# Two experts' outputs kept on chip and summed by one-hot products on TensorE, in a two-layer encoder step

## Chip, cores and metric

The kernel runs on one core of a Trainium2 chip, in one launch. The metric is the time of the program on the device in microseconds, measured before as the median of three runs.

## What is computed

Two layers over 576 rows of 1024 (512 prompt frames, 64 sample frames; padded to five row tiles of 128). Each layer is attention and a gated MLP in parallel, an output projection, a layer norm, a mixture of experts and a second layer norm. Only the experts and the norm behind them matter here. From the reference:

```python
combine = jnp.einsum('tk,tke->te', w, jax.nn.one_hot(idx, N_EXPERTS, dtype=jnp.float32))  # top 2 of 16
y = jnp.zeros_like(xt)
for e in range(N_EXPERTS):
    h = jax.nn.silu(xt @ wg[e]) * (xt @ wu[e])
    y = y + combine[:, e:e + 1] * (h @ wd[e])
...
x = layer_norm(ALPHA * x + y, ln2_g[l], ln2_b[l])
```

## The kernel before

**Products.** A float32 product with weights is made of three fast ones: ScalarE copies a weight unit to `w_hi` (`split_hi`), VectorE subtracts it into `w_lo` (`split_lo`), and TensorE multiplies hi by hi, hi by lo and lo by hi. Each layer has 108 units of up to 1 MB, loaded by SyncE into `raw` and `raw_far`. Products from `pe.matmul` with plain float32 operands (transposes, the gated MLP's) are single.

**Experts.** Each of the 16 experts has 128 places. POOL gathers an expert's rows from `x1_dram`; TensorE makes `gate`, `up` and `down`; ScalarE copies the output from banks C and D to `expert_out` (two buffers, by even and odd expert, `expert_rows_out`); POOL scatters it to `y2_dram` (`send`), row 2r + j for the j-th chosen expert of row r. `out_free` tells ScalarE when a buffer is free. Experts 1 to 14 run in a loop; expert 15 is last, with `down` of 14 and 15 behind it. Where an expert has more than 128 rows, further blocks run in `overflow`; every engine loads the count and branches there. In the profiled execution no block runs.

**Behind the experts**, in each layer:
- ScalarE: `h_hi` of expert 15, the test in `overflow`, in layer 0 splits of units 0 and 1 of the next layer (`next_split`), the last `expert_rows_out`, two more splits, then x times ALPHA for five tiles (`scaled`).
- VectorE: `h_lo` of expert 15, sums of the chosen scores and the weights `w12`, the test, in layer 0 the splits 0 to 2, then `add_first` for five tiles, `add_second` with the row sum, `centre_2` and `normalise` (a centre and a scale operation per tile); `x_ready` tells that a tile is finished.
- POOL: loads of `y_first` tiles 0 and 1 when the last unit is split, the scatter of expert 15, the other loads of `y_first`, and, when the scatter has landed, the loads of `y_second`.
- TensorE: `head(l + 1)`, in layer 0 only: turn a tile of x (`turn_rows`, banks E and F), wait for `xt_hi` and `xt_lo`, the first projection's product (24 instructions) of that tile.
- SyncE: the next layer's w_in, units 0 to 3 as places come free, units 4 on when `x_ready` has come for tile 0.

Banks are filled in a fixed order, which `fill_plan` writes down: a filler waits until the filling before it was read.

## Time and profile before

| what | us |
|---|---|
| median of 3 runs | 1206.39 |
| lowest, highest | 1197.67, 1210.31 |
| profiled execution | 1204.36 |
| its span | 1202.8 |
| busy in the span: TensorE, VectorE, ScalarE, POOL | 1060.8, 890.2, 710.1, 207.6 |

The mean granted clock of TensorE is 0.941 of full speed. The page's line of TensorE's clock over 40 slices of 30 us shows 9 or 8 tenths nearly everywhere, 5 in the slice from 571 us on (between the layers), and 8 and 5 in the last two. Times are read as microseconds from the span's start; layer 0 ends and layer 1 begins at about 571 to 593.

### The profile page before, as it was taken

To read this page: it belongs to the slowest core of one execution; us is meant where nothing else is said; L and a number is where in the kernel's file an instruction comes from. 1 tells how busy PE (TensorE), PEld (TensorE's weight loads), DVE (VectorE), ACT (ScalarE), POOL (GpSimd) and SP (SyncE) were. 2 spreads that over 40 slices of the span, in tenths; PEclk is the share of its full clock that TensorE was granted. 3 is DMA by queue.
4 is the path that set the end of the run, shared out by engine and by line. 5 is a ranking of instruction groups with operands and counts; after the bars stand their busy time and mean duration, and the time that the engine had idled before them with its cause. 6 is when DMAs were issued, how large, how long until landed. Compare 5 with 4: busy or idle time off the path is not lost.

```text
span 1202.8 us, 16880 instructions
## 1 busy us (share of the span) xinstructions
PE 1060.8 (88%) x5460; PEld 888.5 (74%) x5460; DVE 890.2 (74%) x1136; ACT 710.1 (59%) x871; POOL 207.6 (17%) x182
## 2 busy tenths in 40 slices
PE   5999799989989999999289987999799999999950
PEld 4987598877878888887178866888677888888840
DVE  2683865378979988887747737735899798888947
ACT  2423665265768887877433246723577787787852
POOL 3000000014632111210220000100173311222120
PEclk9999889998999999999589988999899999999985
DMA  9523111217999999997824212002499999999934
GB/s 301 160 77 105 51 38 44 88 72 275 356 358 380 388 382 377 381 379 278 251 72 166 61 62 88 27 18 105 134 308 360 378 389 383 379 383 384 378 122 151
DMA packets 117061, 273.26 MB, mean 227 GB/s; under 512 B 10305, under 2 KB 13345, under 8 KB 116993
## 3 DMA queue, kind: packets, MB, share of 16 engines
q1 hardware_dynamic: 98608, 227.36, 52.1%
q0 software_dynamic: 17088, 42.45, 10.6%
q10 hardware_dynamic: 1296, 2.62, 0.7%
q8 instruction: 33, 0.54, 0.2%
q14 instruction: 36, 0.29, 0.1%
HBM read 262.02 MB, written 25.22 MB: 239 GB/s over the span
## 4 chain that ended last, share of the span: by engine, by line
PE 52%; DMA 20%; DVE 10%; issue 6%; ACT 5%; POOL 3%; DVEq 2%; ACTq 0%; SPq 0%; POOLq 0%
DMA raw_far<-in_w_gate 14%; PE bankA L1666 9%; PE bankB L1666 7%; PE bankA L1915 7%; PE bankB L1915 5%; PE bankC L1666 4%; PE bankD L1666 4%; PE bankC L1938 3%; PE bankD L1938 3%; POOL slot_rows L673 3%; DVE w_lo L427 3%; PE bankG L1739 2%; ACT w_hi L421 2%; PE bankE L1655 2%; PE bankF L1655 1%
## 5 line engine op out<-in xcount | busy, mean ns | idle before, releaser
L427 DVE TENSOR_TENSOR w_lo<-raw,w_hi 128x2048 fp32r<-128x2048 f32 (+1 forms) x152 | 340.8, 2262 | 55.5 <-ACT w_hi L421 51.4
L421 ACT ACTIVATE w_hi<-raw 128x2048 fp32r<-128x2048 f32 (+1 forms) x152 | 287.4, 1896 | 138.7 <-PE bankC L1666 46.1
L427 DVE TENSOR_TENSOR w_lo<-raw_far,w_hi 128x2048 fp32r<-128x2048 f32 x64 | 146.4, 2288 | 15.3 <-ACT w_hi L421 15.3
L421 ACT ACTIVATE w_hi<-raw_far 128x2048 fp32r<-128x2048 f32 x64 | 122.8, 1919 | 50.3 <-PE bankB L1915 22.0
L1915 PE MATMUL bankA<-w_hi,xe_hi 128*128 128x512 f32 x256 | 101.8, 398 | 3.8 <-DVE xe_lo L442 3.6
L1915 PE MATMUL bankB<-w_hi,xe_hi 128*128 128x512 f32 x256 | 102.6, 401 | 1.3 <-DVE w_lo L427 1.3
L1915 PE MATMUL bankA<-w_lo,xe_hi 128*128 128x512 f32 x256 | 100.6, 393 | 0.0
L1915 PE MATMUL bankA<-w_hi,xe_lo 128*128 128x512 f32 x256 | 100.6, 393 | 0.0
L1915 PE MATMUL bankB<-w_hi,xe_lo 128*128 128x512 f32 x256 | 100.1, 391 | 0.0
L1915 PE MATMUL bankB<-w_lo,xe_hi 128*128 128x512 f32 x256 | 99.9, 390 | 0.0
L653 POOL DMA_INDIRECT y_rows<-expert_out,idx x32 | 53.2, 1662 | 173.4 <-ACT expert_out L928 171.0
L647 POOL DMA_INDIRECT rows<-x_rows,idx x24 | 37.0, 1541 | 219.6 <-PE bankF L1655 158.0
L1915 PEld LDWEIGHTS bankA<-w_hi,xe_hi 128*128 128x128 f32 x256 | 48.6, 190 | 18.1 <-DVE xe_lo L442 8.0
L1938 PE MATMUL bankC<-w_hi,h_hi 128*128 128x512 f32 x128 | 53.2, 415 | 4.9 <-DVE h_lo L442 4.9
L1915 PEld LDWEIGHTS bankA<-w_hi,xe_lo 128*128 128x128 f32 x256 | 48.6, 190 | 10.4
L1915 PEld LDWEIGHTS bankB<-w_hi,xe_hi 128*128 128x128 f32 x256 | 48.1, 188 | 10.8 <-DVE w_lo L427 1.8
L1915 PEld LDWEIGHTS bankA<-w_lo,xe_hi 128*128 128x128 f32 x256 | 48.6, 190 | 9.7
L1915 PEld LDWEIGHTS bankB<-w_hi,xe_lo 128*128 128x128 f32 x256 | 48.0, 188 | 10.3
L1915 PEld LDWEIGHTS bankB<-w_lo,xe_hi 128*128 128x128 f32 x256 | 48.2, 188 | 9.1
L1938 PE MATMUL bankC<-w_lo,h_hi 128*128 128x512 f32 x128 | 50.7, 396 | 0.0
L1938 PE MATMUL bankC<-w_hi,h_lo 128*128 128x512 f32 x128 | 50.6, 395 | 0.0
L1938 PE MATMUL bankD<-w_hi,h_hi 128*128 128x512 f32 x128 | 50.1, 391 | 0.0
(373 smaller groups left out, 2539.6 us busy)
## 6 DMA issues: line engine op xcount, KB each, us to landing
raw<-in_w_up SPq DMA_DIRECT2D x64, 1024.0 KB, 7.3
raw_far<-in_w_gate SPq DMA_DIRECT2D x60, 1024.0 KB
raw<-in_w_down SPq DMA_DIRECT2D x60, 1024.0 KB, 12.4
raw<-in_w_in SPq DMA_DIRECT2D x12, 1024.0 KB, 6.5
raw<-in_w_o SPq DMA_DIRECT2D x8, 1024.0 KB, 6.2
x_rows<-x POOLq DMA_DIRECT2D x10, 512.0 KB, 3.0
raw<-in_w_gate SPq DMA_DIRECT2D x4, 1024.0 KB
raw_far<-in_w_down SPq DMA_DIRECT2D x4, 1024.0 KB
```

What stands on the lines that cost most here:

```text
L421: act.activation(w_hi[:, s % RB, :, 0:n], raw_unit(s)[:, :, 0:n], ACT.Copy).then_inc(hi_done, 1)
L427: dve.tensor_tensor(w_lo[:, s % RB, :, 0:n], raw_unit(s)[:, :, 0:n], w_hi[:, s % RB, :, 0:n].bitcast(F32), ALU.subtract).then_inc(lo_done, 1)
L647: pool.indirect_dma_start(out=rows[:, e % 2, :], out_offset=None, in_=x1_dram, in_offset=bass.IndirectOffsetOnAxis(ap=src.bitcast(U32), ax ...
L653: pool.indirect_dma_start(out=y2_dram, out_offset=bass.IndirectOffsetOnAxis(ap=idx[:, e, 0:1].bitcast(U32), axis=0), in_=expert_out[:, e % ...
L673: pool.indirect_dma_start(out=slot_dram, out_offset=bass.IndirectOffsetOnAxis(ap=slots[:, c:c + 1].bitcast(U32), axis=0), in_=ints[:, c, : ...
L1655: ins = pe.transpose(bank_of(name)[:, k * P:(k + 1) * P], src, ident)
L1666: ins = pe.matmul(out, a[:, k, col:col + P], w[:, slot, j, 0:n], start=(m == 0 and a is a_hi and w is w_hi), stop=(m == len(steps) - 1 and ...
L1739: ins = pe.matmul(bank_of(("o", t))[:, h * 64:(h + 1) * 64], probs_t[:, j % 2, 2 * a + b, :], v[b], start=(b == (0 if t else 1)), stop=(b ...
L1915: ins = pe.matmul(out, a[:, 4 * k + t, (c % 2) * P:(c % 2 + 1) * P], w[:, (s + k) % RB, t, :], start=(k == t == 0 and a is xe_hi and w is ...
L1938: ins = pe.matmul(bank_of(f"down{h}")[:, :], a[:, 2 * j + r, cols], w[:, (s + j) % RB, 2 * r + h, :], start=(j == r == 0 and a is h_hi and ...
```

## The change

The outputs of experts 14 and 15 are not scattered. They stay in `expert_out`. VectorE makes, for both, a one-hot matrix of each row tile (`own`: a row's place in the expert, times its weight); TensorE turns these (`own_t`), and `own_sum(t)` multiplies them with the outputs into two banks per row tile. VectorE adds the banks to x (`add_own`). In x, rows in these two experts' first 128 places have weight 0 for the fetched output, and `y2_dram` is filled with the input rows ahead of each layer's experts, so that rows never scattered hold finite numbers. The other outputs are loaded by SyncE: `y_second` when the last `up` product is filled, `y_first` when the last unit is split. ScalarE scales x before the test. Row tiles' adds are now: second, first, own.

Cut to its core:

```diff
+    for name, bank in ((("own", 0), "E"), (("own", 1), "F"), (("own", 2), "H")):
+        fill(name, bank)
+    for t in range(NT):
+        for h in range(2):
+            fill(("sum", t, h), ("AB", "CD", "GH", "GH", "GH")[t][h])
     return at, count
...
-        y_second = over(base_m, "y_second", [P, NT, D], at=8 * HALF)
+        y_second = over(base_t, "y_second", [P, NT - 1, D], at=24576)
+        y_second_last = over(base_m, "y_second_last", [P, D], at=4 * D)
...
+                with sp.If(l < DEPTH - 1):
+                    for s in range(RB):
+                        load_proj(l + 1, s, DEPTH - 1)
+                sp.sem_inc(held_sp, 1)
+
+                def load_outputs(j):
+                    for t in range(NT):
+                        n = P if t < 4 else DEC
+                        first = y_first[0:n, t, :] if t < 4 else y_first_last[0:n, :]
+                        second = y_second[0:n, t, :] if t < 4 else y_second_last[0:n, :]
+                        sp.dma_start((first, second)[j],
+                                     y2_dram[2 * P * t:2 * P * t + 2 * n, :].rearrange("(p j) n -> p j n", j=2)[:, j, :]) \
+                            .then_inc((y_first_in, y_second_in)[j][t], 16)
+
+
+                for c in range(2):
+                    sp.wait_ge(out_free[c], (NE // 2) * (l + 1))
+                    sp.sem_inc(held_sp, 1)
+
+                wait_filled(sp, "up", l, 0, NE - 1)
+                sp.sem_inc(held_sp, 1)
+                load_outputs(1)
+
+                sp.wait_ge(lo_done, RX + UNITS * (l + 1))
+                sp.sem_inc(held_sp, 1)
+                load_outputs(0)
 
             for t in range(NT):
 
...
+                for j in range(2):
+                    for r0, n, src in ((0, SEQ, x_prompt[0]), (SEQ, DEC, x_sample[0])):
+                        pool.dma_start(y2_dram[2 * r0:2 * (r0 + n), :].rearrange("(p j) n -> p j n", j=2)[:, j, :], src) \
+                            .then_inc(y2_filled, 16)
+
                 pool.dma_start(table[:, 0:2, :], ln1_g[l].rearrange("(a c) -> a c", a=2).partition_broadcast(P)).then_inc(ln1_g_in, 16)
...
-                def send(e, beside=None):
+                def send(e):
                     for c in range(2):
                         hold(freed["CD"[c]], nth(f"down{c}", l, 0, e) + 1)
                     scatter(e)
-                    if beside is not None:
-                        beside()
-                    hold(out_sent[e % 2], 16 * (l * (NE // 2) + e // 2 + 1))
+                    hold(out_sent[e % 2], 16 * (l * (NE // 2 - 1) + e // 2 + 1))
                     pool.sem_inc(out_free[e % 2], 1)
 
-                for e in range(NE - 1):
+                hold(y2_filled, 64 * (l + 1))
+                for e in range(NE - 2):
                     if e + 4 < NE:
                         gather_next(e + 4)
...
                 hidden_hi(0, NE - 1)
+                act.wait_ge(x1_out, 16 * NT * (l + 1))
+                act.sem_inc(held_act, 1)
+                for t in range(NT):
+                    act.activation(x[:, t, :], x[:, t, :], ACT.Copy, scale=ALPHA).then_inc(scaled, 1)
+
+                def own_out():
+                    for e in range(2):
+                        wait_filled(act, ("own", e), l)
+                        read(act.activation(own_t[:, e, :], bank_of(("own", e))[:, :], ACT.Copy), ("own", e))
+                    wait_filled(act, ("own", 2), l)
+                    read(act.activation(own_t_last[:, :, :], bank_of(("own", 2))[:, 0:2 * P].rearrange("p (e n) -> p e n", e=2),
+                                        ACT.Copy), ("own", 2))
+
+                def last_out():
+                    expert_rows_out(0, NE - 1)
+                    own_out()
+
...
-                    expert_rows_out(0, NE - 1)
+                    last_out()
...
+                dve.tensor_copy(own_iota[:, :], iota_far[:, :])
+                dve.scalar_tensor_tensor(out=own_rank[:, :, :], in0=tiles(pick[:, 0:NT * NE], NT)[:, :, NE - 2:], scalar=-far,
+                                         in1=tiles(bank_of("rank")[:, 0:NT * NE], NT)[:, :, NE - 2:], op0=ALU.mult, op1=ALU.add)
...
                 dve.reciprocal(srec, ssum)
-                dve.drain()
+                hidden_lo(0, NE - 1)
+
+
+                dve.tensor_scalar(own_in[:, :, :], own_rank[:, :, :], float(P) - far, None, ALU.is_lt)
+                dve.drain()
+                dve.tensor_tensor(own_w[:, :, :], tiles(score[:, :], NT)[:, :, NE - 2:], own_in[:, :, :], ALU.mult)
+                dve.drain()
+                dve.tensor_tensor(own_w[:, :, :], own_w[:, :, :], srec.unsqueeze(2).to_broadcast([P, NT, 2]), ALU.mult)
+                dve.drain()
+                for e in range(2):
+                    for t in range(NT):
+                        ins = dve.tensor_scalar(own[:, e, t, :], own_iota[:, :], own_rank[:, t, e:e + 1], own_w[:, t, e:e + 1],
+                                                ALU.is_equal, ALU.mult)
+                ins.then_inc(own_done, 1)
+                dve.tensor_scalar(own_in[:, :, :], own_in[:, :, :], -1.0, 1.0, ALU.mult, ALU.add)
+                dve.drain()
+                for v in (pick1, pick2):
+                    mine = tiles(v[:, :], NT)[:, :, NE - 2:]
+                    dve.tensor_tensor(mine, mine, own_in[:, :, :], ALU.mult)
+                dve.drain()
+                picked(s1, score[:, :], pick1)
+                picked(s2, score[:, :], pick2)
                 dve.tensor_tensor(w12[:, :, 0], s1, srec, ALU.mult)
...
 
-                def add_first(t):
+                def add_sent(t):
                     dve.wait_ge(scaled, NT * l + t + 1)
                     dve.sem_inc(held_dve, 1)
+                    dve.wait_ge(y_second_in[t], 16 * l + 16)
+                    dve.sem_inc(held_dve, 1)
+                    add_output(t, 1, y_second[:, t, :] if t < 4 else y_second_last[:, :])
                     dve.wait_ge(y_first_in[t], 16 * l + 16)
                     dve.sem_inc(held_dve, 1)
+                    dve.drain()
                     add_output(t, 0, y_first[:, t, :] if t < 4 else y_first_last[:, :])
 
-                def add_second(t):
-                    dve.wait_ge(y_second_in[t], 16 * l + 16)
-                    dve.sem_inc(held_dve, 1)
+                def add_own(t):
+
                     n = P if t < 4 else DEC
-                    add_output(t, 1, y_second[:, t, :], accum_out=mv[0:n, t, 0:1])
-                    dve.drain()
-                    dve.tensor_scalar(mv[:, t, 0:1], mv[:, t, 0:1], -1.0 / D, None, ALU.mult).then_inc(mean_done, 1)
+                    for h in range(2):
+                        part = x[0:n, t, h * HALF:(h + 1) * HALF]
+                        wait_filled(dve, ("sum", t, h), l)
+                        read(dve.scalar_tensor_tensor(out=part, in0=bank_of(("sum", t, h))[0:n, :], scalar=1.0, in1=part,
+                                                      op0=ALU.mult, op1=ALU.add, accum_out=mv[0:n, t, h:h + 1]), ("sum", t, h))
+                    dve.drain()
+                    dve.tensor_scalar(mv[:, t, 0:1], mv[:, t, 0:1], mv[:, t, 1:2], -1.0 / D, ALU.add, ALU.mult).then_inc(mean_done, 1)
 
                 def normalise(t):
...
-            def head(l):
+            def head(l, own_sum=None):
 
                 turn_rows(l, 0)
                 for t in range(NT):
+                    if t == 1 and own_sum is not None:
+                        own_sum(NT - 1)
                     if 2 <= t + 1 < NT:
                         turn_rows(l, t + 1)
                     wait_read(pe, ("xt", t, 1), l)
                     projection(l, 0, t)
                     if t == 0:
+                        if own_sum is not None:
+                            own_sum(NT - 2)
                         turn_rows(l, 1)
...
+                for e in range(3):
+                    wait_free(pe, ("own", e), l)
+                    pe.sem_inc(held_pe, 1)
+                pe.wait_ge(own_done, l + 1)
...
+                turn(("own", 2), l, [own[:, e, 4, :] for e in range(2)])
+
+                def own_sum(t):
+                    if t == 0:
+                        pe.wait_ge(freed["H"], nth(("own", 2), l) + 1)
+                        pe.sem_inc(held_pe, 1)
+                        wait_read(pe, "down0", l, 0, NE - 1)
+                        pe.sem_inc(held_pe, 1)
+                        wait_read(pe, "down1", l, 0, NE - 1)
+                        pe.sem_inc(held_pe, 1)
+                    for h in range(2):
+                        wait_free(pe, ("sum", t, h), l)
+                        for e in range(2):
+                            mine = own_t[:, e, t * P:(t + 1) * P] if t < 4 else own_t_last[:, e, :]
+                            ins = pe.matmul(bank_of(("sum", t, h))[:, :], mine, expert_out[:, e, h * HALF:(h + 1) * HALF],
+                                            start=(e == 0), stop=(e == 1))
+                        done(ins, ("sum", t, h))
...
-                overflow(pe, l, past, block_pe, held_pe)
-
+                overflow(pe, l, past, block_pe, held_pe, blocks_sent, own_read)
+
+                for t in range(3):
+                    own_sum(t)
                 with pe.If(l < DEPTH - 1):
-                    head(l + 1)
+                    head(l + 1, own_sum)
+                with pe.If(l > DEPTH - 2):
+                    for t in range(3, NT):
+                        own_sum(t)
```

On ScalarE, between the last expert's `h_hi` (here `h_hi<-bankG`) and the work behind the test of the count, before. L928 is `expert_rows_out`, L1013 the scaling:

```order
L928 ACTIVATE expert_out<-bankC 128x512
L928 ACTIVATE expert_out<-bankD 128x512
L1004 COMPARE_AND_BRANCH
L397 REGISTER_ALU
L413 ISA
L421 ACTIVATE w_hi<-raw 128x4x256 x2
L1004 UNCONDITIONAL_BRANCH
L473 UNCONDITIONAL_BRANCH
L1010 REGISTER_ALU
L1013 ACTIVATE x<-x 128x1024 x5
L1015 ACT_TABLE_LOAD
```

The same place after the change, first from `h_hi` to the test (L478), then what follows in layer 0 when no block runs (L970 is `expert_rows_out`, L1012 and L1014 are `own_out`):

```order
L454 ACTIVATE h_hi<-bankG 128x4x128
L1004 REGISTER_ALU
L1007 ACTIVATE x<-x 128x1024 x5
L478 TENSOR_LOAD count_max
L478 ISA x2
L479 COMPARE_AND_BRANCH
```

```order
L438 ACTIVATE w_hi<-raw 128x2048 x2
L1059 UNCONDITIONAL_BRANCH
L970 ACTIVATE expert_out<-bankC 128x512
L970 ACTIVATE expert_out<-bankD 128x512
L360 REGISTER_ALU
L1012 ACTIVATE own_t<-bankE 128x512
L1012 ACTIVATE own_t<-bankF 128x512
L360 REGISTER_ALU
L1014 ACTIVATE own_t_last<-bankH 128x256
L1063 COMPARE_AND_BRANCH
L414 REGISTER_ALU
L430 ISA
```

The scaling has moved from behind the last splits to ahead of the test, and three copies stand behind the output copy.

On VectorE, from the last unit's split to the weights `w12` (L1549, L1550, on `small`), before:

```order
L427 TENSOR_TENSOR w_lo<-raw_far,w_hi 128x2048
L442 TENSOR_TENSOR h_lo<-bankG,h_hi 128x4x128
L1506 TENSOR_TENSOR work_wide<-score,pick_91 128x80
L1508 TENSOR_REDUCE r_1_106<-work_wide 128x5
L1506 TENSOR_TENSOR work_wide<-score,pick_92 128x80
L1508 TENSOR_REDUCE r_2_107<-work_wide 128x5
L1543 TENSOR_TENSOR r_3_108<-r_1_106,r_2_107 128x5
L1545 TENSOR_TENSOR r_3_108<-r_3_108,small 128x5
L1547 RECIPROCAL r_4_109<-r_3_108 128x5
L1549 TENSOR_TENSOR small<-r_1_106,r_4_109 128x5
L1550 TENSOR_TENSOR small<-r_2_107,r_4_109 128x5
L461 TENSOR_LOAD count_max
```

After, from the middle of the score sums on (L1616 are the one-hots, L1627 the first of `w12`):

```order
L1600 TENSOR_TENSOR r_3_115<-r_1_113,r_2_114 128x5
L1602 TENSOR_TENSOR r_3_115<-r_3_115,small 128x5
L1604 RECIPROCAL r_4_116<-r_3_115 128x5
L459 TENSOR_TENSOR h_lo<-bankG,h_hi 128x4x128
L1608 TENSOR_SCALAR own_120<-own_119 128x10
L1610 TENSOR_TENSOR own_121<-score,own_120 128x10
L1612 TENSOR_TENSOR own_121<-own_121,r_4_116 128x10
L1616 TENSOR_SCALAR own<-own_iota,own_119,own_121 128x128 x10
L1619 TENSOR_SCALAR own_120<-own_120 128x10
L1623 TENSOR_TENSOR pick_98<-pick_98,own_120 128x5x2
L1623 TENSOR_TENSOR pick_99<-pick_99,own_120 128x5x2
L1564 TENSOR_TENSOR work_wide<-score,pick_98 128x80
```

`h_lo` stands behind the sums now, and the one-hots and a second pass over the picks ahead of the weights.

On TensorE in layer 1's head, from the end of the first projection of tile 0 on, before:

```order
L1666 MATMUL bankA<-w_lo,xt_hi 128x512
L1666 MATMUL bankA<-w_hi,xt_lo 128x512
L1689 REGISTER_ALU
L1655 MATMUL bankE<-ident,x 128x128 x4
L1655 MATMUL bankF<-ident,x 128x128 x4
L1689 REGISTER_ALU
L347 REGISTER_ALU
L1655 MATMUL bankE<-ident,x 128x128 x4
L1655 MATMUL bankF<-ident,x 128x128 x4
L1666 MATMUL bankB<-w_hi,xt_hi 128x512
```

After:

```order
L1751 MATMUL bankA<-w_hi,xt_lo 128x512
L364 REGISTER_ALU
L2076 MATMUL bankG<-expert_out,own_t 128x512 x2
L364 REGISTER_ALU
L2076 MATMUL bankH<-expert_out,own_t 128x512 x2
L1774 REGISTER_ALU
L1740 MATMUL bankE<-ident,x 128x128 x4
L1740 MATMUL bankF<-ident,x 128x128 x4
L364 REGISTER_ALU
L2076 MATMUL bankG<-expert_out,own_t_last 128x512 x2
L364 REGISTER_ALU
L2076 MATMUL bankH<-expert_out,own_t_last 128x512 x2
```

`own_sum(3)` stands between the projection of tile 0 and the turn of tile 1, `own_sum(4)` (with `own_t_last`) behind that turn.

## Rows read from the trace of the kernel before

**Rows 1.** The timeline of TensorE, seam of the layers: start us, us, line, operation.
```profile
592.95 1.11 PE L1655 MATMUL bankE<-ident,x 128*128 128x128 f32 x4 [21.93 <-DVE x L1209]
...
608.55 1.11 PE L1655 MATMUL bankE<-ident,x 128*128 128x128 f32 x4 [3.08 <-DVE x L1209]
...
617.81 0.60 PE L1655 MATMUL bankE<-ident,x 128*128 128x128 f32 x4
```

**Rows 2.** The chain that ended last, in order of time: start us, us, what.
```profile
575.32 9.80 DMA y_first_last<-y_rows
...
1169.60 9.80 DMA y_second<-y_rows
```

**Rows 3.** The timeline of VectorE, seam of the layers.
```profile
564.39 0.69 DVE L442 TENSOR_TENSOR h_lo<-bankG,h_hi 128x512 fp32r<-128x512 f32 x1 [2.24 <-ACT h_hi L437]
...
568.86 5.63 DVE L427 TENSOR_TENSOR w_lo<-raw,w_hi 128x2048 fp32r<-128x2048 f32 x3 [1.62 <-issue]
...
586.95 1.29 DVE L1582 SCALAR_TENSOR_TENSOR x<-y_second,small,x 128x1024 f32<-128x1024 f32 x1 [0.19 <-issue]
```

**Rows 4.** The timeline of VectorE, end of layer 1.
```profile
1154.33 0.69 DVE L442 TENSOR_TENSOR h_lo<-bankG,h_hi 128x512 fp32r<-128x512 f32 x1 [2.23 <-ACT h_hi L437]
...
1177.44 1.28 DVE L1582 SCALAR_TENSOR_TENSOR x<-y_second,small,x 128x1024 f32<-128x1024 f32 x1 [0.19 <-issue]
...
1183.79 1.28 DVE L1582 SCALAR_TENSOR_TENSOR x<-y_second,small,x 128x1024 f32<-128x1024 f32 x1
...
1198.12 1.28 DVE L1209 SCALAR_TENSOR_TENSOR x<-x,small,table 128x1024 f32<-128x1024 f32 x1
```

**Rows 5.** The timeline of ScalarE, seam of the layers.
```profile
563.77 0.59 ACT L437 ACTIVATE h_hi<-bankG 128x512 fp32r<-128x512 f32 x1
565.28 3.72 ACT L421 ACTIVATE w_hi<-raw 128x2048 fp32r<-128x2048 f32 x2 [0.92 <-issue]
...
571.05 0.60 ACT L928 ACTIVATE expert_out<-bankD 128x512 f32<-128x512 f32 x1 [0.76 <-PE bankD L1938]
...
573.44 4.83 ACT L1013 ACTIVATE x<-x 128x1024 f32<-128x1024 f32 x5
```

**Rows 6.** Single operations of VectorE: a timeline row, and a tile's group.
```profile
681.19 1.12 DVE L1124 TENSOR_SCALAR gv<-gv,small 128x128 f32<-128x128 f32 x4
...
L1124 DVE TENSOR_SCALAR gv<-gv,small x40: 339/342/351, 70.5 to 682.0; 128x128 f32<-128x128 f32 x40
...
L1196 DVE SCALAR_TENSOR_TENSOR x<-x,bankA x10: 679/686/689, 169.5 to 843.3; 128x512 f32<-128x512 f32 x10
```

**Rows 7.** Stretches: busy time of each engine (count), granted clock, DMA share, GB/s.
```profile
580.00:590.00 10.00, 0.00 (x0) 0.00 (x0) 6.71 (x10) 1.41 (x3) 0.18 (x1) 0.50 0.92 256
600.00:601.00 1.00, 1.00 (x3) 0.77 (x3) 1.00 (x1) 0.00 (x0) 0.00 (x0) 0.54 1.04 381
```

**Rows 8.** TensorE: float32 products on the timeline and the chain, projections on the chain.
```profile
122.92 1.02 PE L1767 MATMUL bankG<-gv,ws_t 128*128 128x512 f32 x2
...
129.63 1.71 PE bankG L1767 x2
...
597.05 7.54 PE bankA L1666 x24
...
618.84 5.48 PE bankC L1666 x24
```

**Rows 9.** The timeline of POOL, first scatter of slots in layer 0.
```profile
294.41 2.88 POOL L673 DMA_INDIRECT slot_rows<-ints,slots  x1 [3.96 <-DVE slots L1516]
```

**Rows 10.** POOL's queue in layer 0, and the mask: its issues, readers and landing.
```profile
95.63 0.56 POOL L623 DMA_DIRECT2D table<-in_ln_g  x1
...
L1153 DVE SCALAR_TENSOR_TENSOR probs<-bankA,mask x10: 678/681/691, 121.5 to 772.6; 128x512 f32<-128x512 f32 x10
...
L795 ACTq DMA_DIRECT2D mask<-in_c_mask x2: 387/395/403, 116.9 to 706.4; - x2
...
DMA to landing us min/median/max: 3.3/3.3/3.3
```

More of the change, by code:

```diff
@@ L258, in build @@
         r5 = [over(base_m, f"r5_{k}", [P, NT], at=3 * QB + 3840 + 32 * k) for k in range(7)]
+        own_rank, own_in, own_w = (over(base_m, f"own_{k}", [P, NT, 2], at=3 * QB + 4064 + 64 * k) for k in range(3))
         local = over(base_m, "local", [P, 2 * NT], at=2 * QB + 8 * D)
@@ L700, in _ @@
                     send(e)
-                def load_outputs(j, tiles):
-                    for t in tiles:
-                        n = P if t < 4 else DEC
-                        first = y_first[0:n, t, :] if t < 4 else y_first_last[0:n, :]
-                        pool.dma_start((first, y_second[0:n, t, :])[j],
-                                       y2_dram[2 * P * t:2 * P * t + 2 * n, :].rearrange("(p j) n -> p j n", j=2)[:, j, :]) \
-                            .then_inc((y_first_in, y_second_in)[j][t], 16)
-                def outputs_last(ran):
-                    load_outputs(0, range(NT))
-                def outputs_early():
-                    hold(lo_done, RX + UNITS * (l + 1))
-                    load_outputs(0, range(2))
-                    send(NE - 1, lambda: load_outputs(0, range(2, NT)))
                 def block_rows(e, b, ran):
@@ L732, in block_rows @@
                         out=y2_dram, out_offset=bass.IndirectOffsetOnAxis(ap=ov_pair[:, 0:1].bitcast(U32), axis=0),
-                        in_=expert_out[:, 0, :], in_offset=None,
+                        in_=ov_out[:, :], in_offset=None,
                         bounds_check=2 * ROWS - 1, oob_is_err=False).then_inc(ov_sent, 16)
                     hold(ov_sent, 16 * (ran + 1))
-                overflow(pool, l, past, block_rows, held_pool, outputs_last, lambda: send(NE - 1), outputs_early)
-                load_outputs(1, range(NT))
+                overflow(pool, l, past, block_rows, held_pool)
+                hold(filled["H"], nth(("sum", NT - 1, 1), l))
+                for c in range(2):
+                    pool.sem_inc(out_free[c], 1)
             pool.wait_ge(kv_out, 16 * 5 * DEPTH)
@@ L1007, in no_blocks @@
                     act.sem_inc(held_act, 1)
[L1009 to L1013 removed]
+                overflow(act, l, past, block_act, held_act, after_blocks, last_out, no_blocks)
                 act.activation(warm[:, 0:1], eps, ACT.Sqrt)
@@ L1574, in block_dve @@
                     dve.wait_ge(ov_pe, ran * PE_STEPS + 7)
[L1575 removed]
+                    dve.tensor_copy(ov_out[:, HALF:D], bank["D"][:, :]).then_inc(ov_dve, 1)
                 overflow(dve, l, past, block_dve, held_dve)
```

52 lines of the change are left out of this document (34 added, 18 removed).

## Prediction

> **What bounds the kernel now.** I read the page's chain of work first, then the timeline of each engine at the two ends of a layer, then the granted clock in short stretches. The middle of both layers is not touched. What the change touches is the seam between layer 0 and layer 1 and the end of layer 1.
>
> At the seam TensorE finishes the last expert at 571.03 and next works at 592.95 [rows 1]. In between the chain of work runs over the last scatter and a load of `y_first_last`, 9.80 us [rows 2]. VectorE is through with its splits, 5.63 us from 568.86, before 575, but the first of its adds of second outputs starts only at 586.95 [rows 3]. At the end of layer 1 it is the same: the last scatter, then a load of 9.80 us [rows 2], and VectorE adds second outputs from 1177.44 on [rows 4]. From there VectorE is the bound: 1183.79 to 1188.03 is one row tile, 4.24 us, and the last operation ends at 1199.3 [rows 4].
>
> So up to 586.95 and 1177.44 the path is data movement; behind these it is VectorE, and at the seam VectorE and TensorE in turn. The change takes the movement away. It also adds work to VectorE, TensorE and ScalarE at exactly these places, so each chain must be followed.
>
> **The seam: ScalarE.** Before, ScalarE copies `h_hi` at 563.77, splits from 565.28 (two in 3.72), copies the last half of the last expert's output at 571.05 and scales x from 573.44, 4.83 us [rows 5]. After, the scaling comes first: 564.4 to 569.2. The test of the overflow count costs 0.92, the idle time ahead of 565.28, so the two big splits run 570.1 to 573.8, the two output copies to 574.9, three copies of the turned one-hots at about 0.5 each to 576.4, the two half splits to 578.3 (half as long each). The output copy that ended at 571.65 thus ends 3.3 us later, and the splits 4.8 us later.
>
> **The seam: VectorE.** The sums of scores, 1.9 us behind `h_lo` before, move into the 2.24 us of idle time before `h_lo` (564.39) and cost nothing. Behind it come three small operations (0.24 each), ten one-hots of 128x128, and nine small ones (2.0 together). The trace has no such one-hot. I price it by the nearest row, a tensor_scalar of the same shape with two column scalars: four in 1.12, so 0.28 each [rows 6] (bounds: 0.24, a small operation, and 0.34, this one alone). The one-hots are ready at 568.6, before TensorE's 571.03, so that wait is free. All are done at 570.6. The test costs VectorE 1.62, its idle time ahead of 568.86 [rows 3], to 572.2. Two big splits of 2.29 follow to 576.8; the third waits for ScalarE's at 577.3 and ends at 578.6. Only then do the ten adds of fetched outputs start. They wait for no load: SyncE issues the second outputs once the last `up` product is filled and the first ones behind the last unit's `w_lo`, 562.15 (where VectorE's 2.24 us of idle time begin). Even if all 4.7 MB started there, the 256 GB/s of the same loads before [rows 7] would bring them by 580.6, tile 0 long before 578.6, and the adds go on slower than the loads.
>
> The adds are 1.28 each, dependent in pairs: 2.5 per row tile, 12.6 in all, to 591.4. The adds from PSUM are two of 0.69 instead of one of 1.28 [rows 6], with the mean 1.7 instead of 1.5. Before, the first finished row tile came 5.9 us behind 586.95 (TensorE's turn, 592.95, waits for it); now it comes 6.3 behind 591.4, at 597.7. **x for the first tile is ready 4.9 us later than before.** The loads did go off the path; the adds they used to be overlapped with came onto it.
>
> **The seam: TensorE.** A float32 product of 128x512 (two records on TensorE) holds the chain for 1.71 at the granted clock of 0.50, which is 1.2 GHz; at 1.00, 2.4 GHz, I take half of it, 0.86, which the 1.02 from start to end at 122.92 bounds above [rows 8]. Each row tile needs four. Three tiles' sums run 576.5 to about 589 (some 5 us of it at 0.50), hidden before 597.7. Then TensorE idles for 8 us and the clock falls again, as it did in the 21.9 us behind 571.03; from 600 to 601 it still was 0.54 [rows 7], 4 us into the first projection [rows 8]. The head so starts at 0.50, as before: turn, `xt_lo`, first projection at 602.2 for 7.5 us [rows 8], to 609.8. Now `own_sum(3)` (3.4) stands before the turn of tile 1, and `own_sum(4)` (3.4) behind it. VectorE waits for `own_sum(3)` from 604 to 611.5 with tile 3, and with it everything of tile 1 and 2. Tile 2 is ready at 618.2, its turn is over at 619.2, and the second projection runs there at the full clock, 5.5 as a later one did [rows 8], since TensorE did not pause: the turn behind it starts at 624.5, where it started at 617.81 [rows 1]. Of the added products' 6.8 us, 3.1 fill the idle gap ahead of 608.55 [rows 1], and 2 come back from the clock. **The seam costs 6.7 us**, and the projections behind it only carry this on.
>
> **The end of layer 1.** No splits here. VectorE: `h_lo` at 1154.33 [rows 4], one-hots done 1158.5, small ones 1160.6, test 1162.2, and a jump over the branch of layer 0 that used to be hidden under the load; it is not to be seen before, its bounds are 0 and the 1.62 of the test, I take 1.0. Adds of fetched outputs 1163.2 to 1175.8. Products: output copied 1161.6, turned one-hots 1163.3, sums of tiles 0 to 2 done at 1173.7, in time. Banks G and H then wait for VectorE's add of tile 2, near 1182; TensorE has idled 8 us and starts `own_sum(3)` at the low clock (half clock for four products). Its second half is ready about 2 us late. With steps of 4.5 instead of 4.25 and this stall the last operation ends at 1200.6, where it ended at 1199.4 [rows 4]: **+1.2 us**. The start is 1.4 earlier (1176.0 for 1177.44); five steps at 0.2 more and 1.6 of stall that is not made up eat it.
>
> The rule of the Trainium skill for control flow (page "Advanced Engine Details and Errata", section Control Flow Timing) is about 51 ns for a branch and 108 ns for compare-and-branch. The rows show 1.62 us for VectorE's test and 0.92 for ScalarE's [rows 3, 5], with what loads the count among it. By the page the test and the jump would be near 0.3 and 0.1, and the whole sum about 3.5 us less, 1209.5; I go by the rows.
>
> **The routing chain.** VectorE gets a copy of 128x128 and a small operation ahead of the slots that POOL's first scatter at 294.41 waits for [rows 9], on the chain to the rows of expert 4. Bounds per layer: 0 and 0.58 (0.34 and 0.24); I take 0.35 for the overlap of independent operations: +0.7 in both.
>
> **The filling of y2.** Four DRAM to DRAM copies a layer, 4.7 MB, go on POOL's queue ahead of `table<-in_ln_g`, at 95.6 in layer 0. The next transfer that is waited for is the mask: issued by ScalarE at 116.9 and 706.4, landed in 3.3, first read at 121.5 [rows 10], slack 1.3. If a copied byte costs as much as a read one, fills and the 2.1 MB of gate weights beside them are over after 18 us (381 GB/s [rows 7]), by 114: no cost. If it costs twice, after 30 us, at 127: then the mask shares the engines. I take nothing, and keep up to 11 us for the range. The two scatters that fall away (0.97 of POOL each) were waited for only at the end.
>
> **Sum.** 6.7 + 1.2 + 0.7 = 8.6 us more. The profiled execution took 1204.4, span 1202.8; that gives 1213.0. It lies 2.0 below the median of the runs shown, 1206.4, whose spread is 12.6; so the same sum on the median would be 1215.0. I keep 1213.0.
>
> **Rivals.**
> *The filling delays the mask* (slower by over 1%). The copies cost twice and the mask is served behind them: it lands near 127 instead of 120.2, 7 us late, less the slack 5.5 in each layer, 11 together: 1224. It decides when the copies run under about 225 GB/s. For it: the queue also carries `ln_g`, and DMA is shared. Against: engines serve several queues at once, the mask is only 0.4 MB. With half of that, 1218.5.
> *The fetched adds are hidden* (faster). If VectorE had finished the ten adds when the first sum is ready, it would go on at 1166.8 (four products behind 1163.3) instead of 1176 and at about 580 instead of 591.4: 9 and 11 us less, 1193. The data is there in time. Against: VectorE's list, where the adds stand behind one-hots, test and splits; to hide, the first must start by 1154, and `h_lo` itself starts at 1154.33.
> *TensorE stays at the high clock into layer 1's head*: the sums run slower, end near 597, and the first projection takes 5.45 instead of 7.5, with the turns 3 us less: 1210.
> *The loads are not early*: they slip behind w_in's units on SyncE. Up to 3 us they have room; beyond that each us counts once. I give it no chance of its own.
>
> **How the numbers follow.** The forecast has 0.60, the filling 0.18, the hidden adds 0.10, the clock 0.12. What a measurement can tell from no change is about 1%, 12 us: faster is below 1194, slower above 1218.5. Faster: the hidden adds, 0.10. Slower: most of the filling, 0.16, and the forecast's own upper part (one-hots of 0.34, jumps of 1.6, layer 1's sums wholly at the low clock, 5 us together), 0.09: 0.25. The rest, 0.65, is no change that can be told. The range: below, clock and cheap one-hots (-5) and the spread of the runs to 1200; above, half to most of the filling, 1222. It leaves out the hidden adds and the worst of the filling.
>
> **What would show it.** Right: scaling on ScalarE at 564; VectorE's ten adds without a wait, beginning near 578.6 and 1163; first work of layer 1 on TensorE near 598; four added products between the first projection and the turn of tile 1; a wait of VectorE for bank G or H in both layers; the granted clock at 0.50 near 1183. Wrong: an add that waits for `y_first` or `y_second`, adds that begin before 575, or first scores that wait for the mask.

## The result, and the profile after

The changed kernel took 1219.57 us (median of 4 runs, 1217.20 to 1224.60), the kernel before 1208.35 beside it (4 runs, 1197.67 to 1211.51). The ratio is 1.0113, 95% interval 1.0078 to 1.0148: slower, by 11 us in the medians (14 in the means), where the forecast was +8.6 and "no change that can be told". The profiled execution took 1217.2, span 1215.6, 12.8 more than before.

To see where, I cut the span at points that both kernels have. The last `h_lo` of layer 0 comes 1.3 us earlier. From it to the last turn of x at the seam (a turn is TensorE's transposing of one row tile) there are 7.1 us more (66.8 for 59.8). From there to the first slot scatter 0.2 more, to the first gather by `idx` 1.7, to the last `h_lo` of layer 1 1.1, and from that to VectorE's last operation 4.0 (49.1 for 45.1). Two places are thus large: the seam and the end of layer 1.

The seam, TensorE's timeline of the changed kernel (start us, us, engine line operation, idle before and what ended it):

```profile
574.09 3.23 PE L2076 MATMUL bankA<-expert_out,own_t 128*128 128x512 f32 x4 [3.22 <-ACT own_t_last L1014]
577.12 2.34 PE L2076 MATMUL bankB<-expert_out,own_t 128*128 128x512 f32 x4
...
584.45 1.88 PE L2076 MATMUL bankH<-expert_out,own_t 128*128 128x512 f32 x4
595.80 1.11 PE L1740 MATMUL bankE<-ident,x 128*128 128x128 f32 x4 [9.48 <-DVE x L1264]
...
608.06 1.88 PE L2076 MATMUL bankG<-expert_out,own_t 128*128 128x512 f32 x4
609.78 1.88 PE L2076 MATMUL bankH<-expert_out,own_t 128*128 128x512 f32 x4
611.49 0.60 PE L1740 MATMUL bankE<-ident,x 128*128 128x128 f32 x4
...
617.23 0.65 PE L1740 MATMUL bankE<-ident,x 128*128 128x128 f32 x4 [1.26 <-DVE x L1264]
```

Six sums are through at 586.3, then TensorE idles 9.48 us for x of tile 0, which is turned at 595.80 where it was 592.95 [rows 1]. `own_sum(3)` pushes the turn of tile 1 to 611.49. VectorE, same stretch:

```profile
563.13 0.69 DVE L459 TENSOR_TENSOR h_lo<-bankG,h_hi 128x512 fp32r<-128x512 f32 x1 [0.40 <-ACT h_hi L454]
...
564.47 2.65 DVE L1616 TENSOR_SCALAR own<-own_iota,own,own 128x128 f32<-128x128 f32 x10
...
570.70 5.63 DVE L444 TENSOR_TENSOR w_lo<-raw,w_hi 128x2048 fp32r<-128x2048 f32 x3 [1.27 <-issue]
576.66 1.28 DVE L1660 SCALAR_TENSOR_TENSOR x<-y_second,small,x 128x1024 f32<-128x1024 f32 x1 [0.33 <-issue]
...
588.24 1.27 DVE L1660 SCALAR_TENSOR_TENSOR x<-y_first_last,small,x 64x1024 f32<-64x1024 f32 x1
...
589.70 0.69 DVE L1680 SCALAR_TENSOR_TENSOR x<-bankA,x 128x512 f32<-128x512 f32 x1
```

No add waits for a load. Where the second adds began at 586.95 [rows 3], the adds of the own sums begin at 589.70, behind one-hots, splits and ten fetched adds. So far it went as forecast. ScalarE, too, scales x at once behind `h_hi`, and the waits for the loads that stood on the chain [rows 2] are gone:

```profile
562.50 0.59 ACT L454 ACTIVATE h_hi<-bankG 128x512 fp32r<-128x512 f32 x1
562.98 4.84 ACT L1007 ACTIVATE x<-x 128x1024 f32<-128x1024 f32 x5
567.72 3.70 ACT L438 ACTIVATE w_hi<-raw 128x2048 fp32r<-128x2048 f32 x2
```

The end of layer 1, VectorE [rows 4]. The idle time of the third row was not expected:

```profile
1163.19 0.69 DVE L459 TENSOR_TENSOR h_lo<-bankG,h_hi 128x512 fp32r<-128x512 f32 x1 [0.40 <-ACT h_hi L454]
...
1169.35 0.17 DVE L1628 TENSOR_TENSOR small<-r,r 128x5 f32<-128x5 f32 x1 [0.26 <-issue]
1176.15 1.28 DVE L1660 SCALAR_TENSOR_TENSOR x<-y_second,small,x 128x1024 f32<-128x1024 f32 x1 [6.64 <-issue]
...
1201.26 0.69 DVE L1680 SCALAR_TENSOR_TENSOR x<-bankH,x 128x512 f32<-128x512 f32 x1 [1.02 <-PE bankH L2076]
...
1210.98 1.28 DVE L1264 SCALAR_TENSOR_TENSOR x<-x,small,table 128x1024 f32<-128x1024 f32 x1
```

For 6.64 us VectorE waits for nothing that a semaphore shows. At the same place of layer 0 ("issue" 1.27, ahead of 570.70) only the test stands; in layer 1 VectorE also jumps over the splits and over the whole tail of layer 0. What DMA did in those microseconds (by queue: packets, MB, share of 16 engines), from 1163 to 1172 and from 1172 to 1176.3:

```profile
q1 hardware_dynamic: 862, 3.08, 103.1%
q14 instruction: 1, 0.01, 0.2%
...
q1 hardware_dynamic: 34, 0.08, 9.2%
q8 instruction: 2, 0.03, 3.4%
q14 instruction: 2, 0.02, 1.9%
```

The engines are full with SyncE's output loads until 1172. Of the packets that load code one goes through beside them, at 1168.2; the others come behind them, at 1172.6, 1173.1, 1175.7 and 1176.2. The trace does not say which engine's code a packet holds. The kernel before has the same jump, but there VectorE was put down as waiting for `y_first` from 1157.2 to 1165.0:

```profile
1165.00 1.28 DVE L1582 SCALAR_TENSOR_TENSOR x<-y_first,small,x 128x1024 f32<-128x1024 f32 x1 [7.83 <-DMA y_first<-y_rows]
```

### The profile page after: what moved, and what is told of

Same layout as the page of the kernel before. It is cut to its first block, busy times and chain, and to the rows that moved or that the text cites. A ratio compares the mean times of both kernels' runs of the same rounds, so it can differ in the third digit from the quotient of the medians.

```text
span 1215.6 us, 17206 instructions
## 1 busy us (share of the span) xinstructions
PE 1104.5 (91%) x5560; PEld 910.6 (75%) x5560; DVE 912.7 (75%) x1210; ACT 712.9 (59%) x877; POOL 189.1 (16%) x166
## 3 DMA queue, kind: packets, MB, share of 16 engines
q10 hardware_dynamic: 1296, 2.62, 0.6%
## 4 chain that ended last, share of the span: by engine, by line
PE 55%; DMA 16%; DVE 11%; issue 7%; ACT 4%; DVEq 4%; POOL 3%; SPq 0%; ACTq 0%; POOLq 0%
DMA raw_far<-in_w_gate 11%; PE bankA L1751 9%; PE bankA L2004 7%; PE bankB L1751 7%; PE bankB L2004 6%; PE bankC L1751 4%; PE bankD L1751 4%; PE bankC L2027 3%; PE bankD L2027 3%; POOL slot_rows L730 3%; DVE w_lo L444 3%; PE bankG L1828 2%; PE bankE L1740 2%; ACT w_hi L438 2%; DVEq L1671 2%
## 5 line engine op out<-in xcount | busy, mean ns | idle before, releaser
L704 POOL DMA_INDIRECT rows<-x_rows,idx x24 | 32.7, 1362 | 225.9 <-PE bankF L1740 163.3
L710 POOL DMA_INDIRECT y_rows<-expert_out,idx x28 | 43.6, 1557 | 144.3 <-ACT expert_out L970 136.9
L2004 PEld LDWEIGHTS bankB<-w_hi,xe_lo 128*128 128x128 f32 x256 | 48.0, 188 | 10.5
L2004 PEld LDWEIGHTS bankA<-w_hi,xe_lo 128*128 128x128 f32 x256 | 48.1, 188 | 10.1
## 6 DMA issues: line engine op xcount, KB each, us to landing
raw<-in_w_up SPq DMA_DIRECT2D x64, 1024.0 KB, 11.4
y_rows<-in_x_prompt POOLq DMA_DIRECT2D x4, 2048.0 KB, 16.5
```

The costliest lines, as they stand in the source:

```text
L704: pool.indirect_dma_start(out=rows[:, e % 2, :], out_offset=None, in_=x1_dram, in_offset=bass.IndirectOffsetOnAxis(ap=src.bitcast(U32), ax ...
L710: pool.indirect_dma_start(out=y2_dram, out_offset=bass.IndirectOffsetOnAxis(ap=idx[:, e, 0:1].bitcast(U32), axis=0), in_=expert_out[:, e % ...
L2004: ins = pe.matmul(out, a[:, 4 * k + t, (c % 2) * P:(c % 2 + 1) * P], w[:, (s + k) % RB, t, :], start=(k == t == 0 and a is xe_hi and w is ...
```

## Experiments

All were timed beside the kernel before. Each profile was cut at the same points; the table has, in us behind the last `h_lo` of layer 0 or 1, what the verdicts rest on. Turn 0 and last turn are the starts of TensorE's turns of the first and last row tile of x, projection 0 is the start of the first projection, and a fetched add is the add of an output that was loaded.

| kernel | seam: first fetched add | turn 0 | projection 0 | last turn | layer 1: first fetched add | VectorE's end |
|---|---|---|---|---|---|---|
| before | 10.6 | 28.6 | 32.7 | 59.8 | 10.7 | 45.1 |
| changed | 13.5 | 32.7 | 36.9 | 66.8 | 13.0 | 49.1 |
| a0 | 13.5 | 32.7 | 36.9 | 67.2 | 13.0 | 49.7 |
| e1 | 16.5 | 42.7 | 46.9 | 76.1 | 13.2 | 58.9 |
| e2 | 13.5 | 32.7 | 36.9 | 63.7 | 12.9 | 47.4 |
| e3 | 13.5 | 32.8 | 37.0 | 66.6 | 7.8 | 44.9 |
| e4 | 7.8 | 29.0 | 38.8 | 67.9 | 7.6 | 44.9 |
| e6 | 13.5 | 23.5 | 33.0 | 59.2 | 7.8 | 44.6 |
| e8 | 13.5 | 32.7 | 36.9 | 66.6 | 12.8 | 49.2 |
| e9 | none | 23.8 | 28.0 | 56.7 | none | 36.3 |
| e11 | 13.5 | 23.5 | 33.0 | 57.4 | 7.8 | 44.6 |
| e12 | 13.5 | 32.8 | 37.0 | 62.3 | 7.8 | 43.2 |

**a0, the changed kernel again.**

> The changed kernel once more, as the base for the runs beside it and as a second profile. In the first profile three places make up the 12.8 us of span: the seam (about +7.5 from the end of the last expert to the last projection), the way from the slots of layer 1 to the rows of expert 4 (+2.1, 6.8 to 8.9), and the end of layer 1 (+4.0, of it 6.64 us in which VectorE waits for no semaphore ahead of its first add at 1176.15). Theory A (all three belong to the change): the second profile shows them within 0.5 us. Theory B (the +2.1 of the routing chain is chance of the DMA): it is not there again, the other two are, and the median stays 11 +- 4 above the kernel before.

1215.39, ratio 1.0115 (1.0067 to 1.0162). Seam and end are there again. The way from the slots to the gather took 40.7 us, after 41.6 in the first profile and 39.8 before; in the others it was 39.5 to 41.9. Theory B holds: the +2.1 is not there again (0.9 here, inside the spread of the others).

**e3, the fetched adds ahead of the branch.**

```diff
-                def tail(more):
-                    dve.wait_ge(table2_in, 32 * l + 32)
-                    ...
-                    for t in range(NT):
-                        add_sent(t)
+                dve.wait_ge(table2_in, 32 * l + 32)
+                ...
+                for t in range(NT):
+                    add_sent(t)
+
+                def tail(more):
```

> The ten adds of fetched outputs stand ahead of the branch that parts the two layers' tails, so that in layer 1 VectorE skips only the three splits ahead of them, and jumps over the other tail behind them, when the loads have landed. Theory 1 (the 6.64 us ahead of the first add in layer 1 are code loads for the far jump, queued behind the output loads that keep the DMA engines over 90% busy until 1172): the first add comes 3 to 5 us earlier, and the jump behind the adds costs 1 to 3 us: layer 1's end 1 to 3 us earlier. Rival 1 (a jump costs as much with idle DMA queues): the idle time moves behind the adds whole, total within 0.5 us. Rival 2 (the idle time is the test of the count, not the jump): it stays ahead of the adds at over 5 us. Layer 0 is unchanged in all of them.

1210.44, ratio 1.0068 (1.0038 to 1.0097), 5 us below a0 on the same chip; the two ratios' intervals overlap, so the reading rests on the rows. VectorE's idle time ahead of the first add of layer 1, and the one behind the adds, where the far jump now is:

```profile
1166.20 1.28 DVE L1660 SCALAR_TENSOR_TENSOR x<-y_second,small,x 128x1024 f32<-128x1024 f32 x1 [1.49 <-issue]
...
1179.87 0.69 DVE L1680 SCALAR_TENSOR_TENSOR x<-bankA,x 128x512 f32<-128x512 f32 x1 [0.71 <-issue]
```

The 6.64 became 1.49 and 0.71; the end is 4.2 to 4.8 us shorter, more than the 1 to 3 expected. Both rivals fall. The test is not the cost. The jump behind the adds costs 0.71, where layer 0, which does not jump there, has 0.16; the output loads are through by then.

**e1, the output loads behind the jump.** The far jump stays where the change has it, but SyncE's loads wait for a semaphore that VectorE raises at its target.

```diff
 def tail(more):
+    dve.sem_inc(at_adds, 1)
 ...
+sp.wait_ge(at_adds, l + 1)
 load_outputs(1)
```

> SyncE's loads of the experts' outputs wait until VectorE stands at the entrance of its tail, that is behind the test and the jump. The kernel as a whole must become slower, since the loads are no longer early; what is read is only when VectorE comes to the entrance in layer 1. Theory 1 (the jump's code loads wait behind the output loads): VectorE reaches it 2 to 3 us behind the last small operation, where the first add of the changed kernel came 6.6 us behind it; the loads are issued by then. Rival (a jump to code that is not there costs over 5 us whatever the DMA does; the code must be fetched from memory either way): 5 to 6.6 us again.

1231.82 in one run; slower, as was expected of late loads. VectorE's last small operation of layer 1 starts at 1174.17, and SyncE, released by its arrival, issues the first load 2.6 us later:

```profile
1174.17 0.17 DVE L1631 TENSOR_TENSOR small<-r,r 128x5 f32<-128x5 f32 x1 [0.26 <-issue]
```

```profile
1176.81 1.91 SPq L591 DMA_DIRECT2D y_second<-y_rows  x4
```

In the changed kernel the same way took 6.8 us (1169.35 to 1176.15). It is the same jump, without the loads ahead of its code, and test and jump are 4.2 us shorter: theory 1 is shown from both sides. How the 4.2 come about is shown in part only. The first packet of the instruction queue q8 moves 1.0 us behind the start of the last small operation here (1175.2) and 3.3 in the changed kernel (1172.6); VectorE goes on 1.6 and 3.5 us behind it. So if these packets are its code, 2.2 us are code that comes late; for the other 1.9, with the loads all but through, no row has a reason.

**e2, the last two sums ahead of the head.**

```diff
-fill(("sum", t, h), ("AB", "CD", "GH", "GH", "GH")[t][h])
+fill(("sum", t, h), ("AB", "CD", "GH", "EF", "EF")[t][h])
 ...
-for t in range(3):
+for t in range(NT):
     own_sum(t)
```

ScalarE copies the two to SBUF, VectorE adds them with one operation each.

> own_sum(3) and own_sum(4) go to banks E and F ahead of the head, ScalarE keeps them in SBUF, VectorE adds them from there. Theory 1 (the four products between projection 0 and the turn of tile 1, and VectorE's 8.75 us of wait for bank G, are a cost of their own): second turn 3 to 4 us earlier than in the changed kernel, end of layer 1 another 1 us earlier (no wait for bank H), 4 to 5 us in all. Rival (the head is bound by VectorE's x and the low clock, the products only fill a gap): under 1.5 us. If TensorE's longer work ahead of the head also keeps the clock at 1.00 for projection 0 (7.5 us at 0.54 before), 2 us more.

1208.20, ratio 1.0038 (1.0007 to 1.0069), 7.2 below a0. The last turn comes 3.2 to 3.6 us earlier and the end 1.7 to 2.3, together 4.9 to 5.9, where 4 to 5 were expected; what the time of the whole shows beyond that I don't ascribe to the edit. Theory 1 holds, the part on the clock does not: TensorE idled only 2.62 us ahead of turn 0, yet the granted clock was 0.55 from 598 to 602 and 0.50 from 602 to 606.

**e4, as e3, with the splits behind x of tile 0.** Its edit moves the three `split_lo` of the next layer from ahead of the adds to behind `normalise(0)`.

> As e3, and the three splits of w_in stand behind the first finished row tile instead of ahead of the adds. Theory 1 (the splits, 5.6 us, lie on the path to x of tile 0 at the seam): x of tile 0 is ready 5 to 6 us earlier, near 590, the first projection then waits for the splits' last w_lo near 596 instead of starting at 600: 3 to 4 us less at the seam, and with one jump fewer 2 to 4 us less in layer 1. Rival (the tiles behind the first are the bound, and they come later by the same 5.6 us): the seam gains under 1 us, since VectorE's work in all is the same.

1213.11, ratio 1.0096 (1.0063 to 1.0129). Turn 0 came 3.7 us earlier, not 5.6, since the first add of `y_first` now waited 2.16 us for its load. But projection 0 started 1.9 later and the last turn 0.7 to 1.1 later. The end of layer 1 is 4.2 to 4.8 shorter, as in e3. At the seam TensorE waited for `xt_lo` of tile 0, which stands behind the splits and tile 1's centring:

```profile
609.80 0.79 PE L1755 MATMUL bankA<-w_hi,xt_hi 128*128 128x512 f32 x1 [7.79 <-DVE xt_lo L459]
```

The rival holds: VectorE's work at the seam is one queue, and what is moved back there is late for the next thing.

**e9, without the ten fetched adds** (the part of 14 experts is left out of the result).

> The ten adds of fetched outputs are left out in both layers (their waits for the loads stay), so the result lacks what 14 of the 16 experts give. Theory (the adds lie whole on VectorE's path to x of tile 0): x of tile 0 is ready 9 to 10 us earlier relative to the last h_lo at the seam (the first sums are then waited for) and the end of layer 1 starts 10 to 12.8 us earlier: 19 to 22 us less than the changed kernel. Rival (behind the seam TensorE is the bound and takes back part of it; the sums and the loads end late): under 14 us.

1189.84 in one run. Turn 0 came 8.9 us earlier, the last turn 10.1 to 10.5, the end 12.8 to 13.4: 23 to 24 us at the two places, above the 19 to 22 of the theory. The ten adds take 12.8 us. At the end of layer 1 all of it is gained. At the seam it is not, since VectorE, come earlier, waits 3.33 us for the load of `y_first_last` and 0.88 for bank D.

**e8, the filling in layer 0 alone.**

```diff
+with pool.If(l < DEPTH - 1):
     for j in range(2):
         ...
-hold(y2_filled, 64 * (l + 1))
+hold(y2_filled, 64)
```

> The filling of y2 is issued in layer 0 alone (POOL skips it in layer 1, where the rows still hold finite numbers of layer 0, taken with weight 0). Theory (the filling costs nothing, its transfers are through before the mask is waited for): within 1.5 us of the changed kernel, and the stretch from the last turn of the head to the first slot scatter of layer 1 as long as before, 256.7 to 260.3 us in the six profiles. Rival (it delays w_gate's, w_o's or the mask's loads in both layers): 2 to 5 us faster, and that stretch 2 to 5 us shorter.

1215.64, ratio 1.0111 (1.0056 to 1.0165): no difference. But the filling is not free of effect. VectorE's first read of the mask in layer 1, in the changed kernel and in e8:

```profile
718.35 0.69 DVE L1208 SCALAR_TENSOR_TENSOR probs<-bankA,mask 128x512 f32<-128x512 f32 x1 [2.09 <-DMA mask<-in_c_mask]
```

```profile
715.49 0.69 DVE L1209 SCALAR_TENSOR_TENSOR probs<-bankA,mask 128x512 f32<-128x512 f32 x1 [1.38 <-PE bankA L1847]
```

Beside the filling the mask lands in 5.0 and 6.5 us (a0 4.6 and 5.7), where it was 3.3 [rows 10]; in e8 it is 5.3 in layer 0, with the filling, and 3.5 in layer 1, without. VectorE's idle time ahead of that read was 1.38 before. It is 0.7 us longer here and 2.2 in layer 0 (a0: 0.3 and 1.4). In layer 0 the read comes at 123.06 for 121.47; at VectorE's read of bank G near 158 (157.72 for 157.50) only 0.2 of this is left.

**e6, a new order.** VectorE: fetched adds of tile 0, own sum of tile 0, fetched adds of tile 1, tile 0 finished, and so on; the branch behind that; the last tile's adds later. TensorE: turn 0, then `own_sum(3)` and `own_sum(4)` in banks A to D.

```diff
+add_sent(0)
 ...
+add_own(0)
+add_sent(1)
+finish(0)
+add_own(1)
+add_sent(2)
+add_sent(3)
 def tail(more):
+    finish(1, 0 if more else None)
+    add_own(2)
+    ...
```

> A kernel built from what the runs so far showed. VectorE adds tile 0's fetched outputs, then tile 0's own sum, and normalises tile 0 among the other fetched adds; all of this stands ahead of the branch that parts the tails; the adds of the last tile come later. own_sum(3) and own_sum(4) run behind the turn of tile 0 in banks A to D and ScalarE keeps them in SBUF. The split of xt for tile 0 waits for the last add that reads the region that it is written to. Theory (what VectorE does ahead of the first x, the products in the head and the far jump are three separate costs): x of tile 0 ready 9 us earlier relative to the last h_lo, the first projection 4 to 5 us earlier and at the clock of 1.00 since TensorE does not idle for 8 us, last projection 10 to 13 us earlier; the end of layer 1 about 6 us shorter than in the changed kernel: 1197 to 1202. Rival (VectorE's total work bounds the seam, the order of it gives back only the latency of the first tile): 3 to 5 us at the seam, 1205 to 1209.

1202.09 beside 1204.80 for the kernel before, ratio 0.9981 (0.9946 to 1.0016); e8, on the same chip, was 13.6 slower. Turn 0 came 9.2 us earlier, projection 0 3.9 earlier and at a granted clock of 1.00, the last turn 7.7 to 8.0, the end 4.5 to 5.1. The theory holds in its direction. Each part is short of it: projection 0 by a little (4 to 5 were expected), the end too (about 6), the last turn most (10 to 13), where TensorE waited for x of tile 3. The time lies at the upper edge of the 1197 to 1202.

```profile
613.44 0.96 PE L1784 MATMUL bankE<-ident,x 128*128 128x128 f32 x4 [3.84 <-DVE x L1280]
```

**e11, as e6, with tile 3 finished ahead of the last tile's adds.**

> e6 with one change of order in the second half of the seam: tile 3 is finished (and xt_lo of tile 2 made in the time that its square root takes) before the fetched adds of the last tile, and ScalarE makes xt_hi of tile 3 before it squares tile 4. In e6 TensorE waited 3.84 us for x of tile 3 at 613.44, ran at the clock of 0.50 behind it, and the last turn began 59.2 us behind h_lo. Theory (the place of these three VectorE operations is the cost): no wait over 1.5 us at the turn of tile 3, last turn at 54.5 to 56, total 3 to 5 us below e6: near 1198, below the kernel before by 0.3 to 0.8%. Rival (the last tile then comes late by the same amount): last turn at 58 or later, within 1.5 us of e6.

1208.58 beside 1206.10 for the kernel before, on another chip than e6; ratio 1.0015 (0.9990 to 1.0039). The wait for x of tile 3 fell to 1.62, but the last turn came only 1.8 us earlier, since now x of tile 4 is waited for:

```profile
624.67 0.65 PE L1795 MATMUL bankE<-ident,x 128*128 128x128 f32 x4 [1.93 <-DVE x L1285]
```

It is between theory and rival at the seam, and no gain in time.

**e12, e2 and e3 together.**

> The edits of e2 (sums of the last two tiles ahead of the head) and e3 (fetched adds ahead of the branch) together and nothing else. If they are separate costs the times add: relative to the last h_lo the last turn at 63.7 (e2) and the end of layer 1 at 47.4 + 44.9 - 49.4 = 42.9, in all 10 to 12 us below the changed kernel, 1203 to 1206. Rival (both free VectorE at the same place, so that the second gives less): end of layer 1 at 44.5 or more.

1208.36, ratio 1.0024 (0.9998 to 1.0050). Last turn 62.3, end 43.2: separate costs, they add. Against the mean of the changed kernel's two profiles they take 4.7 and 6.2 us off, 10.9 in all. The time itself missed the expected 1203 to 1206; but the kernel before took 1206.10 beside it, and 1201.96 beside a0.

None of these kernels is measurably faster than the one before, save e9, which leaves work out. e6, e11 and e12 take back what the change cost, within what the intervals can tell.

## Why the prediction was wrong, point by point

- **The direction and the seam's total were right.** Forecast 6.7, measured 7.1 and 7.5. x of tile 0 was forecast 4.9 us later (4.75 by the times 597.7 and 592.95 that it gives) and is 4.1 (the test cost VectorE 1.27 for 1.62, and ScalarE nothing that shows). Ten one-hots took 2.65, forecast 2.8. The products in the head were worth 1.8 by the forecast (6.7 less 4.9); they cost 3.0, and e2 got back 3.2 to 3.6. The 2 us "back from the clock" did come: from the turn of tile 2 to that of tile 3 it was 9.3 us before, at a granted clock of 0.50 from 608 to 612, and is 6.4 at 1.00 (617 to 623.5). What the forecast lacks lies ahead of that. The first projection took 8.0 us for 7.6, at 0.50 from 595 to 602 and 0.58 to 606, and x of tile 2 came some 0.8 later behind it, so that its turn waited 1.26. So the total is in part luck: turn 0 came 0.6 to 0.8 earlier than forecast, and the head took 1.2 longer.
- **The step that failed is the jump.** "its bounds are 0 and the 1.62 of the test, I take 1.0." Test and jump were 2.6 together in the forecast and 6.64 in the trace. The upper bound is the idle time of a test, a row without a jump; the jump had no row at all, and its cost depends on what the change itself starts, 4.7 MB of loads just ahead of it. The own adds of layer 1 so began 4.3 us later behind `h_lo` than forecast (26.0 for 21.7), and the steps behind them, with a stall for bank H of 1.02 for 1.6 and more, gave 1.5 back: the end cost 4.0 for 1.2. Of the 4.2 us between 8.6 and 12.8 this is 2.8, the seam is 0.4, and 1.0 lies in pieces that differ from profile to profile. With the jump alone put right the sum is 12.6 us; with the end as it was measured it is 11.4.
- **The second step that failed is what a measurement can tell.** "about 1%, 12 us" is the spread of single runs (12.6 us). Four runs beside four had an interval of 0.35% to either side of the ratio, some 4 us. By that the forecast's own 8.6 us, 0.7%, should have been called slower, even with the jump at 1.0.
- **The trace before held a hint.** VectorE's timeline named a load as what ended the 7.83 us ahead of 1165.00, and the DMA queues had three code packets between 1157 and 1162. A jump under a wait is invisible, but not absent. The Trainium skill says it outright (page "Runtime: NRT & Kernel Launch", section Instruction fetch mechanics): a taken branch to a target outside the loaded window has to fetch it by DMA first. The runs agree, and add the price: with idle queues 0.6 us (e3, over layer 0) and 1.0 over the test (e1, 2.64 from the last small operation on, where e3 with the test alone has 1.65), behind the loads 5.1 over the test (6.80 for 1.65). The rule that I did cite, on branch times, speaks of 0.1 us and would have led farther off.
- **The rest of the end of layer 1** went as told: adds of tiles 0 to 2 did not wait, bank H did, and the granted clock was 0.50 from 1190 to 1198.
- **The routing chain** was taken as +0.7 in both layers together. VectorE's list from the first of its small operations to the slots shows 0.1 a layer (289.50 to 293.28 before, 287.67 to 291.58 after; 878.90 to 882.69 and 885.27 to 889.18). In the longer stretch it is not to be seen: from the last turn to the first slot scatter of layer 1 it is 260.3 us for 260.1, and 256.7 to 259.6 in most of the other profiles.
- **The filling** was taken at 0. "First scores that wait for the mask" was named as what would show it wrong, and they do wait, for 0.3 to 2.2 us more than before. The last of layer 0's copies landed near 118, between the 114 and the 127 of the two cases that it had. The rival's mechanism is there, its 11 us are not.
- **Hidden adds**: the rival's price was 9 us less in layer 1 and 11 at the seam; in e9, where they are gone, it was 13, and 9 to 10. As the prediction argued from VectorE's list, they are not hidden.
- **The chances**: slower had 0.25, and most of it hung on the filling. The bound of the jump and the finer measurement should have carried it.

## What to carry to other kernels

A step that used to wait hides everything ahead of it on its engine: when a change takes the wait away, list what that engine still does there, branches too, and give each a cost. Put common code ahead of the branch, so that a far jump comes when the DMA engines are idle (e3); here the jump's code came late behind the loads. To hold the loads back instead makes the jump short, but cost this kernel more than it gave (e1). On an engine that works without a gap, moved work is not hidden; only a change of what its consumers wait for first gains anything.

## What the runs showed of the hardware

The spread of one kernel's times, 10 to 17 us for the kernel before, goes with TensorE's clock: of its 20 runs beside a0 the fastest (1194.83) had a mean granted clock of 0.950 and the slowest (1211.37) 0.938. Part of it lies in a stretch where the clock has no reason in the code. From the first to the last product with `mt`, the output projection's input, in layer 1 the operations are the same in all twelve profiles. In seven of them it takes 93.2 to 93.3 us at a mean granted clock of 1.00, in three (before, e9, e12) 94.8 at 0.98, in the changed kernel's first 96.5 at 0.96, in e11 98.0 at 0.95. The same place of the work in e6 and e11 to within 1 us (e11 is 5.7 us later there; busy us and count of TensorE, its weight loads, VectorE, ScalarE, POOL; then clock, DMA share, GB/s):

```profile
795.00:800.00 5.00, 5.00 (x25) 4.16 (x25) 0.86 (x2) 0.00 (x0) 0.00 (x0) 1.00 0.00 0
```

```profile
800.00:805.00 5.00, 5.00 (x18) 4.32 (x18) 0.75 (x2) 0.00 (x0) 0.00 (x0) 0.50 0.01 3
```

TensorE is busy for all five us in both, yet e11 gets the 1.2 GHz level there and e6 keeps 2.4 GHz. The stretch ahead does not part them: TensorE was busy 3.43 of 5 us in e11 (795 to 800, granted 0.85) and 3.43 of 5 us at the same place of e6 (789.28 to 794.28, granted 1.00). Why the one fell and the other not stays open. So an offset of 1 to 5 us at such a place in a single profile need be no effect of a change.
